# Moving the expert with the most token blocks to the second place of a mixture-of-experts walk

## What is computed

```python
logits = (ht @ router_w + router_b).astype(jnp.float32)
top_val, top_idx = lax.top_k(logits, TOP_K)          # 4 of 32 experts per token
gates = jax.nn.softmax(top_val, axis=-1)
...
xb = h_pad[idx]                                      # the tokens of one expert
u = xb @ w1[e] + b1[e]                               # 1024 -> 2048
y = clamped_swiglu(u) @ w2[e] + b2[e]                # 1024 -> 1024
return y.astype(jnp.float32) * wt[:, None]
```

## Time and profile before

| | us |
|---|---|
| median of 3 runs | 1353.32 |
| lowest and highest run | 1350.18, 1357.76 |
| the profiled execution, its device time | 1358.97 |
| the profiled execution, span from first to last instruction | 1357.1 |
| mean granted TensorE clock of the profiled execution | 0.938 |

### The profile page before, as it was taken

How to read it: one execution, slowest core, us unless ns; L and a number is a source line. 1 busy time by engine, 2 the same in 40 slices (tenths; PEclk the granted TensorE clock), 3 DMA queues, 4 the chain that set the end, 5 groups by cost and what they waited for, 6 DMA issues and landing times.

```text
span 1357.1 us, 28664 instructions
## 1 busy us (share of the span) xinstructions
PE 1203.8 (89%) x8787; PEld 429.6 (32%) x8788; DVE 464.0 (34%) x936; ACT 204.3 (15%) x459; POOL 281.1 (21%) x414
## 2 busy tenths in 40 slices
PE   4989997477999989997989998989999989998883
PEld 1433546322333323322323332323323323332231
DVE  3399545512223323231223322222232223222217
ACT  3124333000111101010111111111101111111111
POOL 3036001111122211221212221211122212221211
PEclk9989997698999999997989999999999999998986
DMA  9775515699857999999997999999167999999966
GB/s 337 295 282 223 216 71 217 257 407 419 330 239 290 419 421 405 383 419 419 420 419 302 391 420 420 369 418 420 33 272 316 418 421 386 383 419 420 418 259 273
DMA packets 80156, 462.95 MB, mean 341 GB/s; under 512 B 11922, under 2 KB 12066, under 8 KB 31488
## 3 DMA queue, kind: packets, MB, share of 16 engines
q1 hardware_dynamic: 52080, 314.72, 57.2%
q10 hardware_dynamic: 17568, 126.14, 22.6%
q0 software_dynamic: 10480, 21.71, 4.5%
HBM read 453.07 MB, written 16.91 MB: 346 GB/s over the span
## 4 chain that ended last, share of the span: by engine, by line
PE 66%; DMA 20%; DVE 7%; issue 4%; ACT 1%; ACTq 0%; POOL 0%; SPq 0%; POOLq 0%; DVEq 0%
PE bank L1610 31%; PE bank L1638 21%; DMA W<-in_expert_w 14%; PE bank L1518 4%; DMA OV<-h_rows,src_cur 2%; PE bank L1619 2%; DVE W L1033 2%; DMA W<-in_w_ada 2%; PE bank L1598 2%; PE bank L1469 2%; PE bank L1439 1%; PE bank L1682 1%; DMA W<-y_rows 1%; PE bank L1585 1%; PE bank L1401 1%
## 5 line engine op out<-in xcount | busy, mean ns | idle before, releaser
L1610 PE MATMUL bank<-W,OV 128*32 128x512 f32 x5056 | 562.0, 598 | 16.7 <-issue 16.7
L1638 PE MATMUL bank<-W,OV 128*32 128x512 f32 x2528 | 319.4, 642 | 45.8 <-DMA W<-in_expert_w 33.7
L1610 PEld LDWEIGHTS bank<-W,OV 128*32 128x32 f32 x5056 | 171.7, 111 | 382.6 <-issue 379.1
L1276 DVE TENSOR_TENSOR OV<-bank,OV 128x512 f32<-128x512 f32 x79 | 54.6, 691 | 373.8 <-PE bank L1610 340.4
L1289 DVE COPY OV<-bank 64x512 f32<-64x512 f32 x79 | 54.7, 693 | 299.2 <-PE bank L1638 297.0
L1638 PEld LDWEIGHTS bank<-W,OV 128*32 128x32 f32 x2528 | 78.1, 115 | 225.5 <-issue 166.4
L637 POOL DMA_INDIRECT OV<-h_rows,src_cur x102 | 103.9, 1019 | 59.9 <-POOL src_cur L632 43.3
L632 POOL COPY src_cur<-OV 128x2 int32 (+1 forms) x51 | 10.9, 215 | 404.6 <-PE bank L1598 404.6
L857 ACT ACTIVATE OV<-OV 128x256 f32<-128x256 f32 x79 | 35.4, 448 | 375.9 <-DVE OV L1278 369.3
L862 ACT ACTIVATE OV<-bank 128x256 f32<-128x256 f32 x98 | 37.6, 384 | 217.4 <-PE bank L1619 175.5
L1619 PE MATMUL bank<-ident,store 128*128 128x128 f32 x196 | 46.6, 320 | 19.9 <-DVE store L1284 14.8
(11 more groups left out here) (278 smaller groups left out, 748.4 us busy)
## 6 DMA issues: line engine op xcount, KB each, us to landing
W<-in_expert_w SPq DMA_DIRECT2D x252, 1024.0 KB, 4.8
W<-in_expert_w ACTq DMA_DIRECT2D x120, 1024.0 KB, 9.3
W<-in_w_ada SPq DMA_DIRECT2D x24, 1024.0 KB, 9.5
W<-y_rows SPq DMA_DIRECT2D x8, 1024.0 KB, 11.9
W<-in_w_in SPq DMA_DIRECT2D x2, 2048.0 KB, 12.3
W<-in_w_out SPq DMA_DIRECT2D x2, 2048.0 KB, 8.8
store<-in_x SPq DMA_DIRECT2D x4, 512.0 KB, 5.4
W<-in_w_in SPq DMA_DIRECT2D x2, 1024.0 KB, 16.1
```

The lines of the kernel that those rows point to most:

```text
L1276: TTo(u_sb[:, hf, :], bank[hf][:, :], b1_cur, ALU.add).then_inc(u_ok[hf], 1)
L1610: last = mm(bank[hf][H * j:H * j + H, :], xT[:, hf, k % QM, H * (k // QM):H * (k // QM) + H], W1[:, slot, k, UW * j:UW * j + UW], start=(k ...
L1638: last = mm(bank[4 + hf][H * j:H * j + H, :], gT[:, hf, r, H * c:H * c + H], W2[:, c, r, HW * piece:HW * piece + HW], start=(c == 0), stop ...
```

## The change

It adds two operations on one column of 32 partitions to the chain that makes the order. `by(6) == by(7)` holds for the expert of rank 0, the one with the most blocks; it is given -2048, which puts it ahead of all but expert 0 (-4096). All others keep their order.

```diff
@@ -1202,6 +1202,8 @@
             link(TS(by(5), by(7), 1.0, 512.0, ALU.is_lt, ALU.mult))
             link(TTo(by(4), by(4), by(5), ALU.add))
             link(TTo(by(4), spread_no[0:E, :], by(4), ALU.add))
+            link(TS(by(5), by(6), by(7), -2048.0, ALU.is_equal, ALU.mult))
+            link(TTo(by(4), by(4), by(5), ALU.add))
             link(STT(by(3), ident[0:E, 0:1], -4096.0, by(4), ALU.mult, ALU.add))
             link(TTo(cmp, exp_i[0:E, 2, :], diag, ALU.mult))
             nc.vector.reduce_sum(steps_by[0:E, :], cmp, axis=AX.X).then_inc(place_ok, 1)
```

## The result

| | before | after |
|---|---|---|
| median us | 1354.18 (1350.18 to 1357.76, 4 runs) | 1366.87 (1364.08 to 1369.12, 4 runs) |
| profiled execution, span us | 1357.1 | 1367.4 |

The ratio is 1.0097 with a 95% interval of 1.0066 to 1.0128: 12.7 us slower, where 12.1 was forecast. The whole interval lies above 1: the change costs time, though under 1%. A total that fits doesn't yet show that its terms do, and here two of them were wrong by several microseconds each, with opposite effects.

The account below looks back on a forecast made before the run. The prediction took the weight stream as the bound: pieces * 2.63 us plus holes where it stands still. 95.2 - 83.5 + 0.4 = +12.1 us on the median 1353.3 gave 1365.4 us, range 1356 to 1376.

Parts of the forecast that it names:

- The two operations: In the chain that makes the order: two more links of 0.18 us, 0.36 us added in full.
- What the expert costs at place 1: Followed from expert 0's last copy to the 7-block expert's end: all behind it 95.2 us later.
- to the first add: From expert 0's last copy to place 1's first add: 10.88 us, from the same place's row; 6.94 to 14 possible.
- place 2: One-block expert behind the 9-block one: 16.03 us, as after the same expert before, waiting for its W2.
- place 3: Two-block expert: 16 pieces of stream, then some 1.8 us for the last quarter of a `down` and the copy; 27.1 us.
- What its leaving place 20 gives: Two holes go, 51.92 us, and the expert's own 12 pieces, 31.6 us: 83.5 us saved.
- The check by holes: Second count: place 1 holes 48 and 20.5 us, less 51.9 at place 20, less 4 at the 7-block expert: +12.6 us.
- A: Rival: the hole at place 1 is no longer than at place 20, 31.4 us; 1348.8 us; chance 0.12.
- B: Rival, faster: the large expert fills TensorE's waits at the start, saving its full 105.0 us; 1344 us; chance 0.05.
- C: Rival, slower still: 9- and 7-block experts too close, first-time full-step code with nothing to hide it; 1373.5 us; chance 0.07.
- D: Rival: the order isn't as said, wrong rank or the 9 stays where it is; 1353.7 us; chance 0.02.
- The price of a piece: In the full weight stream: 2.63 us a piece at 414 GB/s from the rows, not the skill's 358 GB/s.

Follow-up runs that it names:

- even_routing: The kernel before with the routing replaced: tokens spread evenly over the experts, whatever the logits, 64 blocks instead of 79; 1266.25 us, ratio 0.9325.
- after_again: The changed kernel run again unchanged, for more runs and a second profile (6 code loads); 1366.53 us, ratio 1.0080.
- before_again: The kernel before run again unchanged, for a second profile (6 code loads); 1349.63 us.
- before_third: The kernel before run a third time unchanged (6 code loads); 1353.34 us.

## Why the prediction was right, and where it wasn't

**The bound.** "What counts is where the stream stands still" is shown, by the even routing above all and by the table. Between the means of three profiles each, the change adds 13.4 us of holes (108.7 against 95.3) and 13.5 of span. With like code loading it is 9.2 us of holes and 8.9 of span (13 loads), 13.8 and 15.2 (6 loads).

**The two operations.** 0.36 forecast, about 0.4 seen.

**What the expert costs at place 1.** Forecast 95.2. Seen is 521.38 - 421.38 = 100.0, in which the two operations are counted in (the end of place 0 is 0.36 later), so 99.6. By its steps, from the timeline of the profile after:

| step | forecast | seen | |
|---|---|---|---|
| end of place 0 | 284.84 | 285.20 | |
| to the first add | 10.88 | 6.86 | the lower end,'s warm step |
| the 9-block expert | 97.61 | 95.86 | |
| place 2 | 16.03 | 21.37 | **mis-sized**: 5.08 us as the loop's second turn starts |
| place 3 | 27.1 | 31.23 | **mis-sized** |
| place 4 | 80.09 | 80.86 | |

The first step was taken from the row of the same place, but that row belongs to a one-block expert. With one block at place 1 this step takes 10.2 to 13.7 us in eight profiles; with two blocks or more it takes 6.9 or 7.0 in six. The one-block case is code of its own; why it is slower there wasn't tried. The 5 us that I had seen at 309 and used as a bound for place 1 belong to the start of the loop's second turn, and turned up at place 2, which I had copied from a later turn. They aren't the first use of the slot's full-step code, as I had it: after the change place 2 has one block and no full step, and the wait is there. With 6 code loads (`after_again`) place 2 took 14.3 us, without it. At place 3 I let only a quarter of a `down` follow the last weights; but with two blocks, of the second one all follows:

```profile
433.21 4.96 PE L1640 MATMUL bank<-W,OV 128*32 128x512 f32 x24 [4.04 <-DMA W<-in_expert_w]
...
438.53 1.92 PE L1640 MATMUL bank<-W,OV 128*32 128x512 f32 x16
```

The wait for W2 ends at 433.2 (434.1 was forecast), and the last copy is at 440.5: 7.3 us, not 1.8.

**What its leaving place 20 gives.** Forecast 83.5, seen 91.3: behind place 20 the profile after is 1023.89 - 922.40 = 101.5 us late (1.5 us came between place 4 and there, where I had nothing), and at the last copy of place 28 (1284.46 against 1274.28) 10.2. That term was mis-sized. 3.9 of the 7.8 us are the two holes of the four-block expert at place 24 (1.4 and 2.5 us), which vanish with the 9 in this profile (in `after_again` one of 2.6 stays): I had taken the neighbours' holes as fixed. The rest would make a piece 2.96 us instead of 2.63; its cause wasn't tried.

By this pair of profiles the sum is 0.4 + 99.6 + 1.5 - 91.3 = 10.2 us, against 0.4 + 95.2 - 83.5 = 12.1: errors of +4.4, +1.5 and -7.8. With 6 loads (`after_again` against `before_again` and `before_third`) the place with the operations costs 98.9 and 98.0 instead of 95.6, and the saving is 85.8 and 86.0: smaller errors of the same signs. Part of the closeness of 12.1 and 12.7 is luck. The check by holes had no better parts. It had 68.5 us for the two holes at place 1, and 59.9 were seen (42.2 and 17.7); it had the 7's holes shrink by 4, and they grew: against profiles of the same kind of code loading, from 30.8 to 35.0 and 34.7, and from 24.9 and 24.8 to 29.8. Two errors of 8 us cancel there.

**The rivals.** A (a first hole no longer than before) is refuted by the 42.2 us. B is refuted: a saving of over 95.6 would have been needed and at most 91.4 was seen between profiles with like code loading, and the time went up. `even_routing` shows it from the other side: less time with TensorE idle for 13 to 14% of its stretches. The goal that the Trainium skill gives (Perfetto Trace Analysis, "Optimization Strategies" for DMA), to keep the Matmul engine as busy as possible, taken stretch by stretch, doesn't lead to the better order here: in the holes it is busy all the time. Over the whole span its busy share hardly differs, 89% before and 88% after. C was given 0.07; its 1373.5 wasn't measured, but something of it is there: the 7's holes are 4 to 5 us longer behind the 9, and 5 to 8 us of the time hang on where the 7 stands. D is refuted by the nine adds.

**The price of a piece.** The full stretches carry 412 to 418 GB/s here as well, against the 358 of the Trainium skill (DMA: Bandwidth & Descriptors, "Where 436 GB/s comes from"), which is there half of what an HBM stack gives to two cores; this program runs on one. The measurement decides.

No order tried beats the kernel before; the best of the others is 1.0041. Other ideas, as a second slot for W2, weren't tried.

## What to carry to other kernels

Where a stream of weights is the bound, count the time in which it stands still and not the waits of the compute engine: in these runs a large expert costs little where much is still to be loaded when it starts and the experts beside it are small, and it costs more at the front, behind another large one, or ahead of one of three blocks. Price the place that is left as carefully as the place that is taken, neighbours included. When a forecast hits the total, check its terms: errors of 4 and 8 us hid behind a difference of 0.6. And end a sum over a trace at the same event in each profile, not at the same time: a hole of 7.5 us behind the last weights starts at 1303 in one profile and at 1322 in another.

## What the runs showed of the hardware that was not expected

The same program, on the same inputs, loads 13 blocks of code in the first 190 us of the expert stage in one execution and 6 in another. It goes with a wait of about 5 us of TensorE at place 2, and in the kernel before with times of 1359.0 against 1349.6 and 1353.3. The wait is 5.2 us at 309 in before and 5.1 at 388 after the change, with the weight stream full both times (420 and 407 GB/s). With the stream as full, but 6 loads, it is absent (`before_again`, 309.1 to 315.0: 422 GB/s), so the full stream alone isn't its cause. What decides between the kinds stays open. The rows have 0.21 MB for 13 loads, 16 KB each; the Trainium skill (Advanced Engine Details and Errata, "ISA Cache") gives 16 KB as the size of a cache line, and the trace agrees.

The granted TensorE clock was 0.90 and 0.92 on average in the full stretches of the even routing, where TensorE was idle for 13 to 14% of the time, and 1.00 in every hole shown, where it was busy all the time. Around the wait at place 2 it fell at different points: in before it was 0.50 (1.2 GHz, the lower of its two levels) over the 5.17 us of idle time from 309.21; after the change it was 1.00 (2.4 GHz) over the 5.09 us from 387.85 and 0.66 over the 5.06 us of work behind. What this costs in the time wasn't tried.
